# A bidirectional state-space scan: the decay matrices of both directions are added on GpSimd, multiplied by C.B once, and applied in one product a head and tile

## The reference, cut to what matters

```
acum = cumsum(loga)                                   # per head, within a chunk
seg  = exp(where(tril, acum[i] - acum[j], -inf))      # decay matrix
cb   = einsum('bcign,bcjgn->bcijg', cm, bm)           # C.B, one per group, no direction
y_intra = einsum('bcijgr,bcjgrp->bcigrp', seg * cb, v)        # v = dt * x
y_inter = einsum('bign,bgrnp->bigrp', cm_c, s) * exp(acum)    # s: state of earlier chunks
y = y_intra + y_inter          # forward scan + flipped backward scan
...
y = (y_ssd + ssd_d[:, None] * xs) * silu(z)           # skip connection, then gate
```

## Time and profile before

| what | value |
|---|---|
| median of 3 runs | 2189.33 us (2188.45 to 2189.74) |
| the profiled execution, first to last instruction | 2185.7 us |
| PE busy | 1882.4 us (86%) |
| DVE busy | 804.4 us (37%) |
| ACT busy | 507.6 us (23%) |
| POOL (GpSimd) busy | 335.2 us (15%) |
| the scan stage in it | 442 to 539 us |

### The profile page before, as it was taken

The page is one execution under the profiler, slowest core; times in us unless marked ns, Lnnn a source line. Parts: engine busy times, 40 slices in busy tenths (PEclk is TensorE's granted clock), DMA queues, the critical chain, the costliest instruction groups (busy, mean ns, idle before and its releaser), DMA issues.

```text
span 2185.7 us, 32921 instructions
## 1 busy us (share of the span) xinstructions
PE 1882.4 (86%) x14024; PEld 1132.1 (52%) x14024; DVE 804.4 (37%) x1427; ACT 507.6 (23%) x1119; POOL 335.2 (15%) x323
## 2 busy tenths in 40 slices
PE   6999889999999998888889999989999975666565
PEld 3874668745875433333236556677787731212112
DVE  3331757555633010000026877566774300000001
ACT  2452321343012100001023323444442100000001
POOL 1431054322320000000013000054540000000000
PEclk9999999999999999999999999999999998878888
DMA  9321031240239999999993433200004699999997
GB/s 385 142 86 73 5 118 78 119 190 1 89 150 384 428 430 426 429 431 431 428 407 147 169 154 140 103 2 2 2 2 174 233 428 429 430 427 432 430 430 298
DMA packets 46689, 528.07 MB, mean 242 GB/s; under 512 B 3408, under 2 KB 7760, under 8 KB 23120
## 3 DMA queue, kind: packets, MB, share of 16 engines
q1 hardware_dynamic: 44784, 522.56, 57.3%
q10 hardware_dynamic: 1760, 3.42, 0.4%
HBM read 524.91 MB, written 1.05 MB: 241 GB/s over the span
## 4 chain that ended last, share of the span: by engine, by line
PE 53%; DMA 28%; DVE 12%; issue 2%; ACT 2%; DVEq 1%; PEld 1%; PEldq 0%; POOLq 0%; POOL 0%; ACTq 0%; SPq 0%
DMA ring<-in_moe_w 27%; PE bank L1435 12%; PE bank L709 8%; PE bank L820 7%; PE bank L1317 4%; PE bank L1250 3%; PE bank L788 3%; DVE ring L2421 2%; DVE x L2280 2%; PE bank L1036 2%; PE bank L1013 2%; DVE x L2859 1%; PE bank L961 1%; DMA ring<-in_mod_w 1%; PE bank L627 1%
## 5 line engine op out<-in xcount | busy, mean ns | idle before, releaser
L1435 PE MATMUL bank<-ring,xgs 128*32 128x512 f32 x2984 | 374.0, 655 | 129.4 <-DMA ring<-in_moe_w 128.0
L1435 PEld LDWEIGHTS bank<-ring,xgs 128*32 128x32 f32 x2984 | 106.3, 119 | 370.6 <-issue 284.9
L1435 PE MATMUL bank<-ring,hT 128*32 128x512 f32 x1488 | 190.1, 663 | 75.3 <-DMA ring<-in_moe_w 75.1
L820 PE MATMUL bank<-hT,ring 128*128 128x256 f32 (+1 forms) x784 | 232.7, 454 | 2.0 <-ACT hT L1607 1.4
L2700 DVE SCALAR_TENSOR_TENSOR x<-bank,modT,x 128x256 f32<-128x256 f32 x96 | 42.4, 480 | 457.1 <-PE bank L1461 456.9
L820 PEld LDWEIGHTS bank<-hT,ring 128*128 128x128 f32 x784 | 146.6, 190 | 82.3 <-issue 66.8
L1435 PEld LDWEIGHTS bank<-ring,hT 128*32 128x32 f32 x1488 | 52.3, 120 | 199.3 <-issue 152.6
L2280 DVE SCALAR_TENSOR_TENSOR x<-gluR,cols,x 128x256 f32<-128x256 f32 x240 | 116.2, 484 | 16.6 <-issue 0.9
L709 PE MATMUL bank<-hT,ring 128*128 128x256 f32 x432 | 99.9, 381 | 3.7 <-ACT ssd_g L1658 2.2
L709 PEld LDWEIGHTS bank<-hT,ring 128*128 128x128 f32 x432 | 81.1, 190 | 17.9 <-issue 6.2
L3091 POOL MEMSET gluR<- 128x3008 f32 x1 | 2.6, 2610 | 498.9 <-DVEq L2710 498.9
(11 more groups left out here) (573 smaller groups left out, 3026.0 us busy)
## 6 DMA issues: line engine op xcount, KB each, us to landing
ring<-in_moe_w SPq DMA_DIRECT2D x56, 4096.0 KB, 22.8
ring<-in_moe_w SPq DMA_DIRECT2D x28, 2048.0 KB, 21.1
ring<-in_moe_w SPq DMA_DIRECT2D x55, 1024.0 KB, 14.4
ring<-in_mod_w SPq DMA_DIRECT2D x12, 4096.0 KB, 13.4
ring<-in_moe_w SPq DMA_DIRECT2D x12, 3072.0 KB, 22.0
ring<-in_cd_w SPq DMA_DIRECT2D x6, 4096.0 KB, 14.1
ring<-in_ab_w SPq DMA_DIRECT2D x5, 4096.0 KB, 15.3
ring<-in_ab_wo SPq DMA_DIRECT2D x2, 4096.0 KB, 14.9
```

The source lines that it names most:

```text
L820: last = mm(ps[p["no"] % 4][:, p["c0"]:T], w[:, k, :], hT[:, k, p["c0"]:T], start=(k == 0), stop=(k == KD - 1))
L1435: last = mm(ps[banks + s][32 * j:32 * j + 32, :], lhs[s][:, 4 * kh + k, 32 * j:32 * j + 32], piece(g, k, j), start=(kh == 0 and k == 0), s ...
```

## The change

GpSimd gets a step `both_ways`: it adds the two directions' decay matrices of a head in place (16 adds of 128x512). DVE then multiplies the sum by C.B once a head (16 instead of 32) and, in a second instruction behind a drain, adds D times the identity to each of the four tiles (16 scalar_tensor_tensor of 128x512, with `ident` and the matrix as its two tensors). PE applies one right-hand side a head and tile, so `outputs` has one matmul where it had three, and stands one step later. The two skip-block products of GpSimd are gone. The first two steps of `mix_out` move up in GpSimd's queue, from behind the scan to z = 9 and z = 12. `item_add` of items 6 and 7 and four of the gates move a step. Two waits of PE, `gla_zeroed` and `routed`, are removed elsewhere in the program; what they waited for is also ordered by other semaphores on the same path.

```diff
-        SSD_ACC = {z: v for v, z in enumerate([-2, 0, 2, 4, 6, 8, 16, 17, 19, 21, 23, 25])}
-        SSD_EVAC = {9: [0], 10: [1], 12: [2], 16: [3], 26: [4], 27: [5], 28: [6], 32: [7]}
+        SSD_ACC = {z: v for v, z in enumerate([-2, 0, 2, 4, 6, 8, 17, 18, 19, 21, 23, 25])}
+        SSD_EVAC = {9: [0], 10: [1], 13: [2], 17: [3], 26: [4], 27: [5], 29: [6], 33: [7]}
...
-                    for n in range(3 * q, 3 * q + 3):
-                        kind, t = n // 4, n % 4
-                        if kind and t == 0:
-                            pe.wait_ge(sg("ssd_mat"), 4 * k + 2 + kind)
-                        for hp in range(2):
-                            half = slice(64 * hp, 64 * hp + 64)
-                            right = mats[(4 * k + 2 * hp + kind - 1) % 8][:, tiles[t]] if kind else dskI[:, 2 * k + hp, :]
-                            last = mm(ps[k % 4][half, tiles[t]], xs_t[:, k, t, half], right, start=False, stop=True,
-                                      skip_group_check=True, tile_position=(0, 64 * hp))
+                    if q == 0:
+                        pe.wait_ge(sg("ssd_mat"), 2 * k + 2)
+                    for hp in range(2):
+                        half = slice(64 * hp, 64 * hp + 64)
+                        last = mm(ps[k % 4][half, tiles[q]], xs_t[:, k, q, half], mats[(4 * k + 2 * hp) % 8][:, tiles[q]],
+                                  start=False, stop=True, skip_group_check=True, tile_position=(0, 64 * hp))
...
-                for z in range(-4, 32):
+                for z in range(-4, 33):
                     k, q = z // 4, z % 4
                     if q < 2:
                         spreads(k + 1, q)
                     if z in SSD_KV:
                         item_kv(SSD_KV[z])
+                    outputs((z - 1) // 4, (z - 1) % 4)
                     if z in SSD_ACC:
                         item_add(SSD_ACC[z])
-                    outputs(k, q)
                     if z - 1 in SSD_KV:
                         item_inter(SSD_KV[z - 1])
...
-                    for d in range(2):
-                        u = 4 * k + 2 * hp + d
-                        dve.wait_ge(sg("ssd_decay"), u + 1)
-                        V.tensor_tensor(mats[u % 8], mats[u % 8], cbs[k // 4], ALU.mult).then_inc(sg("ssd_mat"), 1)
+                    m = mats[(4 * k + 2 * hp) % 8]
+                    dve.wait_ge(sg("ssd_both"), 2 * k + hp + 1)
+                    V.tensor_tensor(m, m, cbs[k // 4], ALU.mult)
+                    dve.drain()
+                    by_tile = m.rearrange("p (t i) -> p t i", t=NT)
+                    V.scalar_tensor_tensor(by_tile, ident[:, :].unsqueeze(1).broadcast_to([P, NT, P]), dsk[:, 2 * k + hp:2 * k + hp + 1], by_tile,
+                                           ALU.mult, ALU.add).then_inc(sg("ssd_mat"), 1)
...
+                def both_ways(k, hp):
+
+                    if k >= 8:
+                        return
+                    u = 4 * k + 2 * hp
+                    pool.wait_ge(sg("ssd_decay"), u + 2)
+                    G.tensor_tensor(mats[u % 8], mats[u % 8], mats[u % 8 + 1], ALU.add).then_inc(sg("ssd_both"), 1)
+
+                for z in range(-6, 32):
+                    k, q = z // 4, z % 4
+                    if z + 2 in SSD_KV:
+                        item_values(SSD_KV[z + 2])
+                    if z >= -4 and q in (1, 2):
+                        both_ways(k + 1, q - 1)
+                    if z in (9, 12):
+                        mix_out(OUT_MIX[z == 12:][:1])
```

More of the change, by code:

```diff
@@ L946, in outputs @@
                 def outputs(k, q):
-                    if k < 0:
+                    if not 0 <= k < 8:
                         return
[L950 to L953, removed]
-                    for n in range(3 * q, 3 * q + 3):
-                        kind, t = n // 4, n % 4
-                        if kind and t == 0:
-                            pe.wait_ge(sg("ssd_mat"), 4 * k + 2 + kind)
-                        for hp in range(2):
-                            half = slice(64 * hp, 64 * hp + 64)
-                            right = mats[(4 * k + 2 * hp + kind - 1) % 8][:, tiles[t]] if kind else dskI[:, 2 * k + hp, :]
-                            last = mm(ps[k % 4][half, tiles[t]], xs_t[:, k, t, half], right, start=False, stop=True,
-                                      skip_group_check=True, tile_position=(0, 64 * hp))
+                    if q == 0:
[4 more added lines that the diff above has]
+                                  start=False, stop=True, skip_group_check=True, tile_position=(0, 64 * hp))
                     if q == 3:
@@ L1452, in scatter @@
                     done = Q * layer + q
-                    if q == 0 and steps[0] == 0:
-                        pe.wait_ge(sg("routed"), layer + 1)
                     for dt in steps:
@@ L1545, in _ @@
             project_gla()
-            pe.wait_ge(sg("gla_zeroed"), 1)
             pe.wait_ge(sg("proj_evacuated"), copied(GLA_PAIRS, 0))
@@ L2181, in gla_begin @@
                 V.memset(attm[:, :, :, :], 0.0)
-                dve.drain().then_inc(sg("gla_zeroed"), 1)
+                dve.drain()
                 dve.wait_ge(sg("gla_gz"), 2 * GH)
@@ L2680, in route @@
                         V.tensor_copy(gateT[:, s, 2 * half:2 * half + 2, :], ps[5 + half][:, :].rearrange("p (q t) -> p q t", q=2)).then_inc(sg("gates_copied"), 1)
-                dve.drain().then_inc(sg("routed"), 1)
+                dve.drain()
             def experts(layer, streams):
@@ L2824, in scale @@
                     dve.drain().then_inc(sg("head_mixed"), 1)
-                for z in range(-4, 33):
+                for z in range(-4, 34):
                     k, q = z // 4, z % 4
@@ L2980, in mix_h, with mix_out @@
                     pool.drain().then_inc(sg("weights_mixed"), 1)
-            def mix_out():
-                for v, n in OUT_MIX:
+            def mix_out(steps):
+                for v, n in steps:
                     wa, wb = out_weights(2 * v), out_weights(2 * v + 1)
@@ L3027, in ssd, with item_values @@
                 pool.wait_ge(sg("mod_turned"), 3)
-                for v, (g, d, i) in enumerate(SSD_ITEMS):
+                def item_values(v):
+                    g, d, i = SSD_ITEMS[v]
                     t, r0 = ssd_order(d, i), 32 * d + 8 * g
[L3030 to L3033, removed]
                     if v >= 2:
@@ L3172, in _ @@
             ssd()
-            mix_out()
+            mix_out(OUT_MIX[2:])
             gdn()
```

6 lines of the change are left out of this document (1 added, 5 removed).

## The result

Over four runs each, the kernel before takes 2188.89 us (2186.19 to 2189.74) and the changed one 2202.07 (2199.62 to 2205.65). The ratio is 1.0059 [1.0045, 1.0073]: slower by 13.2 us. The forecast was +4.7, with a chance of 0.42 on slower by over 0.2%, and the range ended at 2198.5. So the direction was about as likely as not, and the size lies outside the range.

What follows compares the result with a forecast made beforehand. The prediction took PE's queue, together with the item loop through DVE's scaling, to bound the stage. It summed -17.2 us of PE work and +21.9 of new waits to +4.7, 2194.0 us, with an 8-in-10 range of 2184.5 to 2198.5.

Steps and rivals of the forecast that it cites:

- The walk: Follows each engine's queue through the stage at fixed prices; puts the mean at 543.75 instead of 539.00, 4.75 us later.
- The granted clock in the stage is 1.00, the higher level.: Clock of the profiled stage, 442 to 539 us, in the kernel before; PE rows were priced from its trace.
- PE stands for some 5 us there: PE before item 7's product, waiting for a scaling behind both heads of pair 4; product 5.8 us late.
- PE's work falls by 17.2 us, from 89.9 to about 72.7: Output matmuls in the stage: a third of 25.82 us is left, 8.6 us.
- +21.9 of new waits: Waits added in the stage by the longer path through POOL and DVE, set against 17.2 us less PE work.
- net of +4.7: Stage total: -17.2 us of PE work and +21.9 of new waits, giving 2194.0 us.
- The exclusion: DVE instructions with two SBUF tensors and POOL instructions exclude each other, one by one; the waiting one goes next.
- the very race: Item 1: the second head's POOL add holds DVE's skip addition off to 450.4; it ends at 451.05.
- the first rival: DVE and POOL: exclusion does not bind for the new forms, or collisions fall elsewhere; -4.2, 2185.1 us; chance 0.15.
- The third rival: POOL's adds slower in place, 1.5 to 2.0 us, as DVE cuts in; +7 to +9, 2197; chance 0.10.
- POOL's queue in the middle: From 482.05 on, 11.7 us of POOL work, giving way to DVE for 0.6 four times; ends at 496.1.
- The fourth rival: Stage: PE alone bounds, so all removed PE work is gained; -17.2, 2172.1 us; chance 0.03.

Runs made afterwards that it cites:

- pe_kept_busy: Changed kernel plus overwritten filler matmuls on PE: four before item 1's product, three behind item 6's, five before item 7's; 2196.93 us, ratio 1.0041.
- scale_first_busy: scale_first plus overwritten filler matmuls on PE, three behind item 6's product and four before item 7's; 2190.81 us, ratio 1.0003.
- two_waits_gone: Kernel before without PE's two waits gla_zeroed and routed, nothing else of the change; 2188.26 us, ratio 0.9994.
- mix_in_gap: Changed kernel with its two mix_out steps at z = 6 and 7 instead of 9 and 12; 2202.21 us, ratio 1.0056.
- skip_on_pe: Changed kernel with the skip term back on PE, blocks made by GpSimd ahead of the scan, two products a head and tile; 2193.37 us, ratio 1.0021.
- scale_first: Changed kernel with DVE's item scaling put ahead of the next pair's multiplication and skip addition; 2195.98 us, ratio 1.0023.
- skip_pe_scale_gap_busy: skip_pe_scale_gap plus one and two overwritten filler matmuls on PE at z = 10 and 11; 2192.54 us, ratio 1.0016.
- skip_pe_scale_gap: Changed kernel with skip term on PE, DVE's scaling ahead of the matrices, and mix_out steps at z = 6 and 7; 2188.39 us, ratio 0.9995.
- mix_behind: Changed kernel with the two mix_out steps back behind the scan in GpSimd's queue; 2205.41 us, ratio 1.0081.

## Why the prediction was wrong

The walk can be held against the trace item by item. Starts of the item products, the walk's and those of after less the 3.68 us by which its stage starts later:

| product | walk | after, shifted | late |
|---|---|---|---|
| item 1 | 451.9 | 451.60 | -0.3 |
| item 3 | 462.3 | 464.17 | +1.9 |
| item 5 | 474.35 | 476.89 | +2.5 |
| item 6 | 489.2 | 491.94 | +2.7 |
| item 7 | 500.55 | 502.70 | +2.1 |
| item 8 | 506.4 | 513.75 | +7.4 |
| item 9 | 513.75 | 521.27 | +7.5 |
| item 11 | 526.95 | 534.81 | +7.9 |
| the mean | 543.75 | 552.68 | +8.9 |

**The step that failed** is the sentence "The granted clock in the stage is 1.00, the higher level." It is right of the kernel before, and the walk then priced every PE row at that level, also behind "PE stands for some 5 us there". The table jumps from item 1 to 3 and, most of all, from item 7 to 8, and those are the places of low clock. Their rows cost 1.3 and 6.0 us more than at the higher level: 7.3 of the 8.9 that the walk misses. The same step stands in the sum as "PE's work falls by 17.2 us, from 89.9 to about 72.7": measured it is 90.5 in the stage. Against it the +21.9 of new waits was too high; PE stands 12.7 us longer. The net of +4.7 thus came from two terms that were both too large. pe_kept_busy and scale_first_busy show the cause by what they change: filling PE, with no wait shortened, gives back 5.1 and 5.2 us. The Trainium skill (TensorE: Matmul & The Clock Gate, "HAM oscillation") describes a matmul kernel whose TensorE waits for a DMA between its tiles: in that wait it is put back to its lower clock, and it begins the next tile slow. By that rule the trace agrees at the stop of 3.77, though the wait is one for DVE (the clock is 1.00 from 454 to 455 and 0.50 from 456 on). At the stop of 4.19, which begins at 502.2, the clock was down already. The twin windows above, with the same idle time and two outcomes, the rule doesn't settle.

**The rest of the walk**, point by point:

- PE's work. The windows of the new output line, for the whole stage, PE and PEld busy:

```profile
446.00:556.40 110.40, 13.73 (x128) 6.72 (x128) 0.89 0.18 76
```

128 records as foretold, but 13.73 us and not 8.6: four records (both heads, one tile) take 0.37 on the chain and 0.63 at the lower clock, where twelve in a row had taken 0.81, 0.27 for four. That is 0.1 too little in the walk, 32 times or 3.2 us. Half of the 32 groups stand on the chain that ended last, so some 1.6 us of it are on the path: about what the clock leaves open of the 8.9.

- The exclusion held, also for the form with the broadcast identity. DVE at item 1 and in the middle, then POOL's side of the first:

```profile
451.36 1.51 DVE L2774 TENSOR_TENSOR x<-x 128x512 f32<-128x512 f32 x1 [1.79 <-POOL x L3033]
452.94 1.59 DVE L2777 SCALAR_TENSOR_TENSOR x<-ident,dsk,x 128x512 f32<-128x512 f32 x1
...
479.07 0.75 DVE L2777 SCALAR_TENSOR_TENSOR x<-ident,dsk,x 128x512 f32<-128x512 f32 x1
...
490.18 2.82 DVE L2774 TENSOR_TENSOR x<-x 128x512 f32<-128x512 f32 x1 [1.85 <-POOL x L3033]
...
496.19 2.68 DVE L2777 SCALAR_TENSOR_TENSOR hT<-ident,dsk,hT 128x512 f32<-128x512 f32 x1
```

```profile
452.73 1.26 POOL L3033 TENSOR_TENSOR x<-x 128x512 f32<-128x512 f32 x1 [0.41 <-ACT x L1987]
```

The skip addition alone takes 0.75. Issued at 452.94 beside POOL's add, which ends at 453.99, it ends at 454.53, 0.54 behind it: the very race that the walk set down for item 1. So the first rival fell. The Trainium skill (GPSIMD Engine Reference, Specifications) names contention between the two engines for DVE instructions with two SBUF inputs. The rows agree and add its size, up to a whole instruction of the other (2.82 at 490.18, behind a `mix_out` step from 490.10 to 492.45).

- The adds: 1.27 undisturbed, as priced; 1.71 at 492.40, and the `wv` products 1.45 to 1.49, the `mix_out` step 2.79, where DVE's instructions stand between them. The third rival's mechanism is there, on this queue alone, and the walk had allowed for it (0.6 four times): from the first add of pair 3 to the second of pair 4 the queue takes 13.3 us, where the walk had 14.05.

- POOL's queue in the middle ends, with the second add of pair 4, at 502.2, 498.5 shifted, where the walk had 496.1. It began 3.15 us later than in the walk, at 488.88 or 485.2 shifted, behind items that were late already. The stop that it named as "some 5 us" at item 7 is 2.18 and 4.19, with a short piece between them.

- The stage's shift passes on one for one: 13.7 in the stage, 13.2 in the runs. The two waits cost nothing, by two_waits_gone.

The fourth rival, PE alone as the bound, was given 0.03 and is nowhere to be seen: PE has fewer matmuls and the stage grew.

**What stays open.** What makes a stop lose the clock in one execution and not in another. Item products behind stops, in the kernels above: 1.10 behind 2.28, 2.33 and 2.43, but 2.05 behind 2.32; 1.10 behind 3.46 (with the clock at 0.52 from 500 on, 1.4 us later), 2.05 behind 3.48, 1.68 behind 3.61, 1.62 to 2.05 behind 3.71 to 4.23. The stop just ahead is thus not the whole of it. In some of these the clock fell while PE stood (mix_in_gap, item 7), in the change it had fallen before the stop began. And the parts can't be added cleanly: skip_on_pe and scale_first give 8.7 and 6.1 us, together 9.2; most likely each counts part of the same lost clock. The split of 7.3 and 6.4 is read from one execution, and takes the same rows at the higher clock as the measure.

## What to carry to other kernels

When a change takes work from TensorE and gives it to a chain that TensorE waits for, price each new stop twice: by its length, and by all the work behind it at the lower clock, which here was about half of the loss (7.3 of 13.7). Look at what stands in the queue between the instruction that TensorE waits for and that one's own input, and take it in front. Judge repairs together: seven that left a stop of 3.46 us or more somewhere in the stage stayed slower than the kernel before. Level with it were the one that left nothing over 1.51 us (0.9995) and scale_first_busy (1.0003), whose long stop was filled. Short stops are no warrant: skip_pe_scale_gap_busy has the same 1.51 and is slower (1.0016 [1.0003, 1.0028]).

## What the runs showed of the hardware

- More TensorE work can shorten a program: scale_first with 7 filler products is 5.2 us shorter than without (4.4 by the ratios).
- The clock also falls without a stop: 0.76 and 0.81 at 488 to 496 in skip_pe_scale_gap, in a stretch with no idle time over 0.25 us; in pe_kept_busy 0.65 at 492 to 496, likewise.
- The granted clock ahead of the stage differs from one profiled execution to the next, in code that is the same (0.50 at 212 to 216 us in some, 1.00 in others), and the stage's start by up to 4.4 us. The dips at 212 don't explain all of that: with one the stage starts at 442.89 in skip_pe_scale_gap, without one at 444.97 in mix_behind. A stage is to be compared from its own start.
- A scalar_tensor_tensor of 128x512 with a broadcast SBUF operand counts as one with two SBUF tensors towards GpSimd: 0.75 alone, 1.59 and 2.68 beside it.
